# Normed tokens ahead of the FFN: turned by crossbar DMA instead of TensorE, modulated in place by VectorE instead of ScalarE

## The reference, cut to what matters

```
x_mid = layer_norm(ALPHA * x + gate1 * mix, ln1_g, ln1_b)
h2    = layer_norm(x_mid) * (1 + scale2) + shift2          # scale2, shift2: one value per channel
x_new = layer_norm(ALPHA * x_mid + gate2 * ((silu(h2 @ Wg) * (h2 @ Wu)) @ Wd), ln2_g, ln2_b)
```

## Time and profile before

| | |
|---|---|
| median of 3 runs | 941.21 us (941.09 to 942.17) |
| the profiled execution | 942.09 us, its span on the slowest core 940.5 us |
| span of the 8 cores | 935.1 to 940.5 us |
| PE busy | 890.6 us, 95% of the span |
| DVE, ACT, POOL busy | 471.4, 334.4, 465.9 us |
| granted PE clock | 0.991 of full speed on the slowest core |

### The profile page before, as it was taken

The page is one execution under the profiler, slowest core; times in us unless marked ns, Lnnn a source line. Parts: engine busy times, 40 slices in busy tenths (PEclk is TensorE's granted clock), DMA queues, the critical chain, the costliest instruction groups (busy, mean ns, idle before and its releaser), DMA issues.

```text
span 940.5 us, 15818 instructions; the slowest of 8 cores (935.1 to 940.5 us)
## 1 busy us (share of the span) xinstructions
PE 890.6 (95%) x5397; PEld 427.1 (45%) x5397; DVE 471.4 (50%) x983; ACT 334.4 (36%) x496; POOL 465.9 (50%) x458
## 2 busy tenths in 40 slices
PE   0789999999999999999999999999999999999995
PEld 0344555555554444444444444444444444444442
DVE  3156647778767223765446554333355433332256
ACT  0043576766655222366432343111144111111132
POOL 9145865322222646799965675333166533423124
PEclk9989999999999999999999999999999999999998
DMA  8998445584643676733865335655556665544013
GB/s 172 176 216 247 122 84 90 84 153 72 110 64 71 143 166 121 163 100 91 183 141 136 73 104 128 125 120 102 76 152 159 152 116 129 114 89 90 23 45 135
DMA packets 52287, 113.77 MB, mean 121 GB/s; under 512 B 4976, under 2 KB 6256, under 8 KB 52208
## 3 DMA queue, kind: packets, MB, share of 16 engines
q0 software_dynamic: 28016, 54.47, 36.8%
q1 hardware_dynamic: 24192, 58.29, 19.5%
HBM read 156.71 MB, written 8.39 MB: 176 GB/s over the span
## 4 chain that ended last, share of the span: by engine, by line
PE 86%; DMA 8%; POOL 1%; issue 1%; DVE 1%; ACT 1%; DVEq 0%; SPq 0%; POOLq 0%; ACTq 0%
PE psum L596 79%; DMA arena<-wqk 5%; DMA arena<-xh 2%; PE psum L792 2%; PE psum L826 2%; POOL arena L585 1%; PE psum L903 1%; PE psum L693 1%; ACT arena L796 1%; PE psum L808 1%; PE psum L841 0%; PE psum L635 0%; PE psum L729 0%; DVE arena L608 0%; DVE arena L888 0%
## 5 line engine op out<-in xcount | busy, mean ns | idle before, releaser
L596 PE MATMUL psum<-arena 128*128 128x512 bf16 (+2 forms) x3752 | 797.2, 370 | 1.9 <-DVE arena L888 0.8
L596 PEld LDWEIGHTS psum<-arena 128*128 128x128 bf16 x3752 | 354.0, 98 | 411.5 <-issue 19.2
L944 ACT ACTIVATE arena<-psum 128x512 f32<-128x512 f32 x88 | 52.4, 595 | 289.6 <-PE psum L596 285.8
L945 DVE TENSOR_TENSOR arena<-psum,arena 128x512 bf16<-128x512 f32 x88 | 60.8, 690 | 180.8 <-PE psum L596 166.3
L926 POOL TENSOR_TENSOR arena<-arena 128x512 bf16<-128x512 f32 x88 | 110.9, 1269 | 65.2 <-DMA arena<-wff 54.6
L608 DVE BATCH_NORM_STATS2 arena<-arena 128x6 f32<-128x512 f32 x120 | 81.4, 689 | 47.2 <-DMA arena<-xh 20.9
L796 ACT ACTIVATE arena<-psum 128x1024 bf16<-128x1024 f32 x80 | 79.5, 1023 | 37.9 <-PE psum L792 37.0
L585 POOL DMA_DIRECT2D arena<-wff x44 | 33.6, 765 | 118.0 <-PE psum L596 116.8
L868 DVE SCALAR_TENSOR_TENSOR arena<-arena,psum 128x512 f32<-128x512 f32 x64 | 43.7, 684 | 70.4 <-PE psum L596 69.8
L612 POOL TENSOR_TENSOR arena<-arena 128x1 f32<-128x1 f32 x68 | 37.5, 559 | 64.9 <-DVE arena L611 63.2
L864 ACT ACTIVATE arena<-psum 128x512 f32<-128x512 f32 x64 | 38.3, 599 | 83.3 <-PE psum L596 83.3
(11 more groups left out here) (94 smaller groups left out, 657.6 us busy)
## 6 DMA issues: line engine op xcount, KB each, us to landing
arena<-wff SPq DMA_DIRECT2D x88, 256.0 KB, 4.0
arena<-wff POOLq DMA_DIRECT2D x44, 512.0 KB, 6.6
arena<-xh SPq DMA_DIRECT2D x30, 512.0 KB, 5.4
arena<-wada POOLq DMA_DIRECT2D x24, 512.0 KB, 9.8
arena<-wc POOLq DMA_DIRECT2D x16, 768.0 KB, 9.4
out<-arena SPq DMA_DIRECT2D x15, 512.0 KB, 2.8
arena<-wout SPq DMA_DIRECT2D x8, 512.0 KB, 4.5
arena<-xh POOLq DMA_DIRECT2D x4, 512.0 KB, 41.0
```

The costliest lines, as they stand in the source:

```text
L596: r = e.matmul(out, lhsT=pairs[i][0], rhs=pairs[i][1], start=(i == 0), stop=(i == n - 1))
L944: G.op('act', lambda e: e.activation(out=sg, in_=ps[0], func=AF.Silu))
L945: G.op('dve', lambda e: e.tensor_tensor(out=ab(i)[:, fi, tok], in0=ps[1], in1=sg, op=ALU.mult))
```

## The change

The eight transposes of a tile on PE and their two PSUM banks go. In their place SP issues one DMA that turns 128 tokens by 1024 channels of `xn` and writes it to its place in `h2T`, without scale and shift. After every second tile DVE applies scale and shift in place, with 8 instructions of 128x256 bf16 from SBUF to SBUF. The late sums `c2(8)` to `c2(15)` alternate between banks 4 and 5 instead of using bank 4 alone. The eight units of the first two FFN rounds are ordered by token group: the four of `tg` 0, then the four of `tg` 1.

```
+    def turn_dma(dst, src):
+
+        return G.op('sp', lambda e: e.dma_start_transpose(out=dst, in_=src))
+
...
         p = t % 2
-        tb = (5, 7)
-        for h in range(2):
-            def f(e, h=h):
-                pt = bkb(tb[h]).rearrange('p (c t q) -> p c t q', c=4, t=2)
-                for c in range(4):
-                    r = e.transpose(pt[:, c, p], xn[:, (4 * h + c) * 128:(4 * h + c + 1) * 128], ident)
-                return r
-            G.op('pe', f, dur=4 * 0.058)
+        turn_dma(h2T[:, :, t * 128:(t + 1) * 128], xn)
         if p:
             for c in range(8):
-                pt = bkb(tb[c // 4])[:, (c % 4) * 256:(c % 4 + 1) * 256]
-                G.op('act', lambda e, c=c, pt=pt: e.activation(
-                    out=h2T[:, c, (t - 1) * 128:(t + 1) * 128], in_=pt, func=AF.Identity,
-                    scale=mcol(3, c, 0), bias=mcol(2, c, 0)))
+                hp = h2T[:, c, (t - 1) * 128:(t + 1) * 128]
+                G.op('dve', lambda e, c=c, hp=hp: e.tensor_scalar(
+                    out=hp, in0=hp, scalar1=mcol(3, c, 0), scalar2=mcol(2, c, 0), op0=ALU.mult, op1=ALU.add))
...
-    B4 = Banks(4)
+    B4 = Banks(4, 5)
...
+    todo[0] = [todo[0][k] for k in (0, 1, 4, 5, 2, 3, 6, 7)]
```

## The result

| | before | changed |
|---|---|---|
| median | 941.69 us (941.09 to 942.21) | 947.3 us by the ratio (two executions) |
| ratio | 1 | 1.006 [1.0044, 1.0076] |
| profiled execution | 942.09 us | 947.36 us |
| span of the slowest core | 940.5 us (core 3) | 945.8 us (core 5) |

A forecast was written before the change was run, and what follows sets the result against it. PE was taken as the bound, with POOL as full where tiles are normed. Terms -7.2 - 0.6 + 2.0 + 3.9 + 2.6 + 6.0 + 1.5 = +8.2 us gave 949.4 us as a median, range 934.5 to 956.

The forecast's parts named there:

- 16 turns off PE: On PE's chain: 128 transposes in 16 turns of 0.45 us each fall away, -7.2 us.
- waits of late sums before: At 453.12 us, tile 9's second late sum waits for the one bank; two banks remove this, about -0.6 us.
- ahead of tile 11 and first modulations: PE waits 1.4 us ahead of tile 11 and 0.6 us for the first four modulations: +2.0 us (0 to 4).
- tiles 0 and 1: DVE's modulations wait for POOL; `c1_unit`'s second sum bank is free after 13.4 us, PE needs it after 9.5: +3.9 us.
- tiles 2 and 3: DVE's modulations wait for POOL, 8.9 us in all against PE's 6.3 us of cover before it wants the bank: +2.6 us.
- tiles 4 and 5: POOL waits for ACT close by, and PE has units of `tg` 0 with free banks: 0 us.
- tiles 6 and 7: No cover, PE's next matmul reads the result; 6.9 us if DVE is let in last, 5.1 at the lower end: +6.0 us.
- tiles 8 to 15: POOL is busy two thirds of the time, nobody needs the result soon, but sums queue behind: +1.5 us (0 to 5).
- the first rival: DVE is let in at POOL's next boundary and keeps the ports for all eight modulations: 937.1 us, chance 0.30.
- The second rival: The bf16 modulation does not meet POOL at all and only PE's work counts: 934.5 us, chance 0.10.
- POOL falls behind too: POOL waits for statistics behind DVE's eight modulations and is shut out while they run: 956 us, chance 0.10.
- The DMA: Turning DMAs on SP's queue land in 4.0 us, hidden from PE up to 9 us; 10.4 adds 1.0 us.

## Why the prediction was right

Forecast 949.4 us, measured 1.006 or 947.3: right in sign and mechanism, and within 2.1 us. Term by term (waits and clock on core 5 of the changed kernel):

| step | forecast | measured |
|---|---|---|
| 16 turns off PE | -7.2 | none on PE; without modulation -7.0, on ACT -8.8 |
| waits of late sums before | -0.6 | 1.4 on core 5 before, 0.3 left |
| ahead of tile 11 and first modulations | +2.0 | 0.96 ahead of tile 11; the rest is part of 4.49 |
| tiles 0 and 1 | +3.9 | 1.49 + 0.96 = 2.45 |
| tiles 2 and 3 | +2.6 | 3.12 |
| tiles 4 and 5 | 0 | 0 |
| tiles 6 and 7 | +6.0 | 4.49 |
| tiles 8 to 15 | +1.5 | 0 |
| granted clock | not in the sum | +3.1 |

*The waits* came to 11.0 us where the four terms and the 2.0 gave 16.0. The mis-sized term is what DVE waits for. I had let it in last, or one at a boundary; here it gets one or two in at each boundary of two compute instructions, so a group lasted 7.10, 7.04 and 7.18 us where PE waited for it, against a forecast of 8.5 for tiles 0 and 1. At tiles 6 and 7 I had given 5.1 as the lower end "if it gets one instruction in at each boundary"; that is the case that came, with 4.49. My ground for "last" was the 1.88 us one of the earlier trace rows, which let POOL's next instruction pass; but that one began during a DMA issue of POOL, as the row says and as every one in the count above did. At tiles 2 and 3 POOL has such an issue: there one L906 took 4.44 us and let POOL go from L896 on to L922, and the wait of 3.12 is the only one above its term. So the first rival (let in and keeps the ports for all eight) is wrong, and the forecast carried over to all boundaries what these traces show only behind a DMA issue.

*The late tiles* cost 0 rather than 1.5: PE is 50.00 of 50 us busy from 500 us on. But with PE not delayed ahead of them the late groups alone cost some 2 us (-6.0 against -7.9 by the same spans for modulation on ACT, in another session), and in the old order PE waits 6.6 behind one of them. Their price hangs on PE's lead.

*The clock* was missing from the sum. After each of the two waits over 3 us the granted clock fell, in the window behind the first and in the one that holds the end of the second:

```profile
440.00:445.00 5.00, 4.80 (x16) 1.93 (x17) 3.30 (x7) 1.74 (x2) 5.00 (x6) 0.69 0.44 126
475.00:480.00 5.00, 3.26 (x9) 1.20 (x10) 5.00 (x9) 0.00 (x0) 3.25 (x4) 0.72 0.27 52
490.00:495.00 5.00, 5.00 (x25) 2.24 (x23) 2.20 (x4) 1.84 (x2) 4.95 (x6) 1.00 1.19 166
```

A fraction of 0.7 is a mix of the levels 2.4 and 1.2 GHz. In PE's timeline above 120 matmuls took 27.48 us, where at 0.216 each they take 25.9; 378 took 83.43 in place of 81.6. The end of a run adds 0.16 us at full clock too (60 matmuls in 13.11 us, 16 in 3.61), so the clock's part is 1.4 + 1.7 = 3.1 us, and nothing behind the waits of about 1 us. So two waits of 7.6 us together cost 10.7.

*The sum* is best taken on one core, since PE is not at the same place on all cores of before at 380 us. On core 5 it has made 1256 matmuls of 512 columns by then, before and changed. Until 620 us it made 1072 before and 1042 in the changed kernel: 30 x 0.216 = 6.5 us behind, and its span went from 939.2 to 945.8 us. The terms give the same: 7.2 us of turns less, 1.1 us of waits for late sums less (1.4 before, 0.3 left), 11.0 us of waits and 3.8 us of slower matmuls and ends of runs more, +6.5. The times compare another pair: the slowest core of before is core 3, which is 8 matmuls or 1.7 us behind its own core 5 at 380 us and had the longest span, 940.5. That accounts for spans of the slowest cores only 5.3 us apart. My 949.4 was nearer than it deserved: waits over by 5.0, clock under by 3.1.

*The rule on ports.* The Trainium skill, "SBUF — State Buffer", section "Who interferes with whom", was the ground of the contention. The runs agree as to who collides: SBUF to SBUF held for up to 8.19 us, from PSUM 397 to 411 ns, ACT 583 to 600 beside a full POOL, and the form with an accumulator 522 to 541.

*The second rival* (the bf16 form doesn't meet POOL) is wrong by the mean of 649 against a minimum of 304 ns. Its price of 934.5 was good, though: it is what the forms that don't meet POOL gave (0.993 and 0.9907). *POOL falls behind too* is true in part, 42.43 of 50 us. Beyond 956 the time went only without the order, to a ratio of 1.0229 and 963 us by the median of before, with waits of 4.91 and 6.58 us behind modulations and a clock of 0.88 to 0.94; how much of that is POOL's delay was not separated.

*The DMA* was hidden, as forecast. Landings of the 16 turns in the changed kernel:

```profile
L592 SPq DMA_TRANSPOSE arena<-arena x16: 1217/1228/2470, 393.5 to 582.7; - x16
...
DMA to landing us min/median/max: 3.0/3.6/10.3
```

3.6 us at the median where I took 4.0, and 10.3 at the most, inside the ends of 2.6 and 10.4. The 10.5 us, the estimate from the figure for one square in the Trainium skill, "VectorE: DVE Perf Modes", section "The three transpose paths", is about the longest of 16 and no typical one. The cover is thin, though: with the new order and one bank on ACT PE did wait 1.6 us for the turned tiles. That the order and the second bank are worth 7 us together beside the turn by DMA stands nowhere in my prediction: the 64 matmuls of `tg` 0 are in its cover of 38.0 us, but what they are worth was never worked out.

## What to carry to other kernels

Before work moves to DVE, ask for each instruction whether it is SBUF to SBUF and what POOL does beside it: a 0.3 us operation became as long as POOL's neighbour, 2.35 us here, and behind a DMA issue of POOL as long as what followed, 4.44 or 8 us. The same work from PSUM, in a form with an accumulator or on ACT, though slower by itself (0.40, 0.54 and 0.59 us), ran beside a full POOL undisturbed, and on ACT turned a loss of 0.6% into a gain of 0.9%. And a reordering that is worth nothing alone (1.0002) was worth 5 us beside the turn by DMA and 16 with the modulation on DVE: such parts are judged together.

## What the hardware showed that I had not expected

- Who is let in follows a pattern: between two adjoining large instructions of POOL one of DVE's starts, two where POOL has a 128x1 instruction between them; one that starts during a DMA issue of POOL can be passed by two large ones (4.44 us) or four (7.94 to 8.19 us), at the same place on all cores.
- Successive L906 start 0.26 us apart when POOL is idle, though each lasts 0.33: two overlap. A group of eight takes 2.09 us then.
- In place on 128x256, bf16 took 304 ns at the least where f32 took 294 (the f32 ones only multiply, the bf16 ones multiply and add): half the bytes bought nothing here.
- The turning DMA holds SP's queue for 1.22 us, where the issue of an ordinary load takes 0.33; the one at 451.01 in the old order on ACT held it for 4.10.
- After a wait of 4.85 us in that kernel the next 8 matmuls took 3.57 us, where 8 behind a wait of 1 us took 1.89; the granted clock was 0.50 from 461 to 464.5 us, the 1.2 GHz level.
